# One more pair of contraction tiles per column pair in seven products, and another way to the sums of weights, in the down projection of a hybrid layer

## The reference, cut to what matters

```python
D_MODEL, SEQ, D_FF = 2048, 256, 5632

def conv_ffn(h, w_up, conv_w, conv_b, w_down):
    S = h.shape[1]
    u = h @ w_up
    up = jnp.pad(u, ((0, 0), (CONV_WIDTH - 1, 0), (0, 0)))
    u = sum(conv_w[j] * up[:, j:j + S] for j in range(CONV_WIDTH)) + conv_b
    a, b = jnp.split(u, 2, axis=-1)
    return (jax.nn.silu(a) * b) @ w_down

h = rms_norm(x, ffn_norm[l])
x = x + conv_ffn(h, w_ffn_up[l], ffn_conv_w[l], ffn_conv_b[l], w_ffn_down[l])
```

## Time and profile before

| | |
|---|---|
| median of 3 runs | 1081.04 us (1080.7 to 1081.21) |
| the profiled execution's own time | 1081.17 us |
| its span in the trace | 1079.4 us |
| PE busy in the span | 1074.4 us (100%), 6543 matmuls |
| PEld | 929.6 us (86%) |
| DVE | 906.8 us (84%) |
| ACT | 634.2 us (59%) |
| POOL | 85.4 us (8%) |
| granted TensorE clock | full speed in all slices |

### The profile page before, as it was taken

The page is one execution under the profiler, slowest core; times in us unless marked ns, Lnnn a source line. Parts: engine busy times, 40 slices in busy tenths (PEclk is TensorE's granted clock), DMA queues, the critical chain, the costliest instruction groups (busy, mean ns, idle before and its releaser), DMA issues.

```text
span 1079.4 us, 18186 instructions
## 1 busy us (share of the span) xinstructions
PE 1074.4 (100%) x6543; PEld 929.6 (86%) x6543; DVE 906.8 (84%) x1370; ACT 634.2 (59%) x930; POOL 85.4 (8%) x120
## 2 busy tenths in 40 slices
PE   9999999999999999999999999999999999999998
PEld 9888888888888888888888888888888888888887
DVE  7878988889756678888888888888878889999997
ACT  7677666757454655545555555555555566656663
POOL 4500100000000000000000000000000000000000
PEclk9999999999999999999999999999999999999999
DMA  8656879787889989888987988889798789789883
GB/s 276 181 162 198 201 231 237 210 225 219 244 262 268 242 269 232 236 251 251 248 245 243 243 242 259 228 246 292 238 257 233 213 292 335 266 309 330 273 308 143
DMA packets 191376, 265.49 MB, mean 246 GB/s; under 512 B 9797, under 2 KB 144086, under 8 KB 191062
## 3 DMA queue, kind: packets, MB, share of 16 engines
q1 hardware_dynamic: 173014, 217.81, 61.5%
q0 software_dynamic: 15616, 41.95, 19.9%
q10 hardware_dynamic: 2688, 5.00, 1.2%
HBM read 259.74 MB, written 46.92 MB: 284 GB/s over the span
## 4 chain that ended last, share of the span: by engine, by line
PE 99%; DVE 0%; issue 0%; DVEq 0%
PE bank L1824 38%; PE bank L1832 20%; PE bank L2219 7%; PE bank L2217 7%; PE bank L2218 7%; PE bank L2070 3%; PE bank L1871 3%; PE bank L1873 3%; PE bank L2072 3%; PE bank L1872 3%; PE bank L2071 3%; PE bank L1792 1%; PE bank L1900 1%; PE bank L2109 0%; PE bank L1797 0%; PE bank L1989 0%
## 5 line engine op out<-in xcount | busy, mean ns | idle before, releaser
L794 ACT CAST w_hi<-raw 128x1024 fp32r<-128x1024 f32 x299 | 312.8, 1050 | 254.3 <-PE bank L1832 114.8
L1203 DVE TENSOR_TENSOR w_lo<-raw,w_hi 128x1024 fp32r<-128x1024 f32 x299 | 364.2, 1223 | 107.7 <-ACT w_hi L794 107.2
L1824 PE MATMUL bank<-hs,w_hi 128*128 128x512 f32 x1792 | 423.0, 391 | 0.0
L1824 PEld LDWEIGHTS bank<-hs,w_hi 128*128 128x128 f32 x1792 | 331.3, 188 | 66.3 <-issue 0.9
L1832 PEld LDWEIGHTS bank<-hs,w_lo 128*128 128x128 f32 x1792 | 224.6, 191 | 5.6 <-issue 0.2
L1832 PE MATMUL bank<-hs,w_lo 128*128 128x256 f32 x1792 | 227.3, 283 | 0.0
L1173 ACT CAST hi_slot<-slot 128x1024 fp32r<-128x1024 f32 (+1 forms) x102 | 118.0, 1187 | 65.7 <-DVE slot L1749 23.5
L1730 DVE TENSOR_TENSOR slot_lo<-slot,hi_slot 128x1024 fp32r<-128x1024 f32 (+1 forms) x102 | 136.7, 1388 | 6.6 <-ACT hi_slot L1173 5.5
L2219 PE MATMUL bank<-hi_slot,gated 128*128 128x512 f32 (+1 forms) x194 | 75.1, 387 | 0.0
L2217 PE MATMUL bank<-hi_slot,gated 128*128 128x512 f32 (+1 forms) x194 | 75.1, 387 | 0.0
L1648 DVE SCALAR_TENSOR_TENSOR C<-U,cols,C 128x256 f32<-128x256 f32 x176 | 73.4, 480 | 0.0
(11 more groups left out here) (249 smaller groups left out, 1178.8 us busy)
## 6 DMA issues: line engine op xcount, KB each, us to landing
raw<-in_w_ffn_up_dram SPq DMA_DIRECT2D x176, 512.0 KB, 5.4
u_sums<-in_w_ffn_down_dram POOLq DMA_DIRECT2D x72, 512.0 KB, 6.8
raw<-in_w_in_dram SPq DMA_DIRECT2D x51, 512.0 KB, 4.7
slot<-u_sums SPq DMA_DIRECT2D x80, 256.0 KB, 5.9
slot<-in_w_ffn_down_dram SPq DMA_DIRECT2D x38, 512.0 KB, 5.1
raw<-in_w_in_dram SPq DMA_DIRECT2D x66, 256.0 KB, 3.5
raw<-in_w_out_dram SPq DMA_DIRECT2D x32, 512.0 KB, 5.8
slot<-in_w_ffn_down_dram SPq DMA_DIRECT2D x32, 256.0 KB, 4.2
```

The source lines that it names most:

```text
L794: act.copy(w_hi[:, i, :], raw[:, i, :]).then_inc(units_hi, 1)
L1203: dve.tensor_tensor(w_lo[:, i, :], raw[:, i, :], w_hi[:, i, :].bitcast(F32), ALU.subtract)\
L1824: m = pe.matmul(banks[b][:, :], w_hi[:, i, c], hs[:, 4 * i + k, :], start=(first and k == 0), stop=(final and k == 3))
```

## The change

It turns one eight of each column pair into a seven, so that 17 of 22 k-pairs are sevens instead of 16. Column pair 0 has 17 sevens in a row. In column pair 1, three runs of sevens (six, six, five) stand between eights, and the last seven is step 20 instead of 19. Three k-pairs' activation sums are parked instead of two, used in turns 6 to 8 of the sevens instead of 5 and 6, and x2's parts are loaded later. The weight sums are the same but made otherwise: in DRAM lie sum 1 = B11 + B12 and sum 2 = B21 + sum 1 for every k-pair, sum 3 = B11 + B21 for nine of 17. VectorE makes sum 3 for the others as sum 2 - B12 and sum 4 as sum 2 + B22, which do not depend on each other. POOL issues 86 transfers instead of 80, one in three units instead of three in ten, with a pause of eight units at unit 30. Piece "b" takes its two weight blocks from two tiles (rows of 2 KB) instead of one (4 KB). Small tiles move into shared ones.

```diff
-PATTERNS = ["CCCCSSSSSSSSDSSSSSSSSc", "CcSSSDSSSSSSSDSSSSSSCc"]
+PATTERNS = ["CCCCSSSSSSSSSSSSSSSSSc", "CcSSSSSSDSSSSSSDSSSSSc"]
-SECOND_SUM_IN_DRAM = tuple(range(0, 16, 2))
-LAST_PARKED_TURN = 6
+THIRD_SUM_IN_DRAM = tuple(range(0, 17, 2))
+LAST_PARKED_TURN = 8
-FIRST_SUM_QUAD = Q_F0
-SUM_STEP = (10, 3)
+SUM_STEP = (3, 1)
+FIRST_SUM_UNIT, SUM_PAUSE = 20, (30, 38)
-        X2_BACK_AT = [[5, 14, 17, 20], [13, 15, 17, 19]]
+        X2_BACK_AT = [[15, 17, 19, 20], [14, 16, 18, 19]]
...
-                sp.dma_start(raw_of(q, "a")[:, 0, :], w_down_v[:, 2 * n, out_columns(pair, 1)]).then_inc(a_loaded, 16)
-                sp.dma_start(raw_of(q, "a")[:, 1, :], u_sums_v[n, 1, :, pair, :]).then_inc(a_loaded, 16)
+                sp.dma_start(raw_of(q, "a")[:, 0, :], u_sums_v[n, 0, :, pair, :]).then_inc(a_loaded, 16)
+                sp.dma_start(raw_of(q, "a")[:, 1, :], w_down_v[:, 2 * n + 1, out_columns(pair, 0)])\
+                    .then_inc(a_loaded, 16)
                 wait_for_slot(q, "b")
-                sp.dma_start(raw_of(q, "b")[:, 0:2, :].rearrange("p b m -> p (b m)"),
-                             w_down_v[:, 2 * n + 1, out_both(pair)]).then_inc(b_loaded, 16)
-                sp.dma_start(raw_of(q, "b")[:, 2, :], u_sums_v[n, 0, :, pair, :]).then_inc(b_loaded, 16)
+                sp.dma_start(raw_of(q, "b")[:, 0:2, :], w_down_v[:, 2 * n:2 * n + 2, out_columns(pair, 1)])\
+                    .then_inc(b_loaded, 16)
+                sp.dma_start(raw_of(q, "b")[:, 2, :], u_sums_v[n, 1, :, pair, :]).then_inc(b_loaded, 16)
...
-                    dve.tensor_tensor(t2, t1, b21, ALU.add).then_inc(t2_made, 1)
-                    dve.wait_ge(t2_made, second_sums_made(q))
-                dve.tensor_tensor(t4, t2, b22, ALU.add).then_inc(t4_made, 1)
+                    dve.tensor_tensor(sum_3, sum_2, b12, ALU.subtract)
+                dve.tensor_tensor(sum_4, sum_2, b22, ALU.add).then_inc(sums_of_block_made, 1)
```

More of the change, by code:

```diff
@@ L429, in seven_of, with third_sum_in_dram, third_sums_loaded @@
             return pair * SEVENS + SEVEN_AT[pair].index(at)
-        def second_sum_in_dram(q):
+        def third_sum_in_dram(q):
             pair, at = divmod(q, QUADRUPLES)
-            return is_seven(pair, at) and K_PAIR_AT[pair][at] in SECOND_SUM_IN_DRAM
-        def second_sums_loaded(q):
-            n = sum(second_sum_in_dram(m) and SLOT_OF[m] == SLOT_OF[q] for m in range(OLD_RING, q + 1))
+            return is_seven(pair, at) and K_PAIR_AT[pair][at] in THIRD_SUM_IN_DRAM
+        def third_sums_loaded(q):
+            n = sum(third_sum_in_dram(m) and SLOT_OF[m] == SLOT_OF[q] for m in range(OLD_RING, q + 1))
             return 16 * n
-        def second_sums_made(q):
-            return sum(is_seven(*divmod(m, QUADRUPLES)) and not second_sum_in_dram(m) for m in range(q + 1))
         def pieces_of(q):
@@ L751, in wait_for_step @@
             def wait_for_step(step):
-                pool.wait_ge(units_used, FIRST_SUM_QUAD * RING + step * SUM_STEP[0] // SUM_STEP[1] + RING)
+                unit = FIRST_SUM_UNIT + step * SUM_STEP[0] // SUM_STEP[1]
+                if unit >= SUM_PAUSE[0]:
+                    unit += SUM_PAUSE[1] - SUM_PAUSE[0]
+                pool.wait_ge(units_used, unit + RING)
             def column_block(tile, c):
@@ L1733, in sums_of_weights @@
             def sums_of_weights(pair, at):
-                q, s = q_of(pair, at), seven_of(pair, at)
-                b21, b22, t1 = [raw_of(q, "b")[:, m, :] for m in range(3)]
-                t2, t4 = [raw_of(q, "c")[:, m, :] for m in range(2)]
+                q = q_of(pair, at)
+                b12, b22, sum_2 = [raw_of(q, "b")[:, m, :] for m in range(3)]
+                sum_3, sum_4 = [raw_of(q, "c")[:, m, :] for m in range(2)]
                 wait_for_down(dve, q, "b")
-                if second_sum_in_dram(q):
-                    dve.wait_ge(second_sum_loaded[SLOT_OF[q]], second_sums_loaded(q))
+                if third_sum_in_dram(q):
+                    dve.wait_ge(third_sum_loaded[SLOT_OF[q]], third_sums_loaded(q))
                 else:
```

67 lines of the change are left out of this document (31 added, 36 removed).

## The result

| | before | after |
|---|---|---|
| median of 11 runs each, one beside the other | 1081.06 us | 1084.42 us |
| lowest to highest | 1080.7 to 1082.26 | 1082.61 to 1087.44 |
| the profiled execution | 1081.17 us | 1083.33 us |
| its span | 1079.4 us | 1081.6 us |

The ratio is 1.0034 (95% interval 1.0026 to 1.0041): slower by over 0.2%. Two things stand out: the profiled execution is 1.1 us faster than the median, and the times lie three times as far apart as before.

The account below looks back on a forecast made before the run. It took TensorE, never starved in the down projection, as the bound, with VectorE nearly as full: 1081.17 - 1.36 + 2.11 + 0.8 = 1082.7 for the profiled execution, 1082.6 us for the median, range 1081.2 to 1084.2.

Parts of the forecast that it names:

- The matmuls that go: Down projection on TensorE: one product less per column pair, 6 matmuls at 0.2269 us, all on the path, -1.36 us.
- What costs nothing: Earlier stages: six more GpSimd transfers, the third parked set and moved small tiles fall where TensorE never waits, 0 us.
- one late unit: Earlier stages: if the cover failed, it would cost about what a landing wait does, up to 0.9 us.
- The tail: End of the kernel: VectorE's merge is no longer hidden, so the last addition starts 0.75 us later; +2.11 us.
- Behind it are the same stores: End of the kernel: after VectorE's last addition the stores were taken as unchanged, with no cost of their own.
- VectorE against TensorE: Down projection: VectorE loses its lead in the runs of sevens and TensorE stalls, +0.8 us, between 0 and 2.6.
- the cap: Down projection: landing loads cap VectorE's lead, so a kernel with less lead meets these waits less; argued against a 2.6 us stall.
- (2): Column pair 0's 17 sevens: VectorE falls behind as landing waits come as before, stall 2.6 us, 1084.4 us; chance 0.20.
- (3): Down projection: VectorE's two sums stay 0.72 us apart, 1.3 us more stall, 1083.9 us; chance 0.10.
- (1): Down projection: the whole gain arrives, 1.36 us less TensorE work is 1.36 us less time, 1079.7 us; chance 0.09.

Follow-up runs that it names:

- before_earlier: The kernel before with one of GpSimd's 80 transfers, the accumulating one due at unit 113, moved to unit 112; 1081.95 us, beside 1081.31 for the kernel before.
- one_later: The changed kernel with one of GpSimd's 86 transfers, the accumulating one due at unit 112, moved to unit 114; 1082.31 us, ratio 1.0008.
- look3: The changed kernel with nothing altered, one more profiled execution; 1086.53 us.
- doubled: The changed kernel with one more GpSimd transfer, a plain 512 KB copy straight behind the accumulating one of unit 112; 1085.77 us, ratio 1.0043.

## Why the prediction was wrong, step by step

**The matmuls that go: right.** 1.36 us, and the kernels without the other costs show it.

**What costs nothing: this is the step that failed.** It put GpSimd's transfers at nothing, under a cover, "stretches where TensorE never waits and VectorE idles 107.7 us ahead of its splits", and bounded one late unit by 0.9. The cover is an average over the stages. At 370 us there is none, as two rows of the kernel before, which the prediction did not look at, show:

```profile
370.27 1.28 DVE L1611 TENSOR_TENSOR xt<-xt,bank 128x512 f32<-128x512 f32 x2
```

```profile
371.60 1.09 PE L1792 MATMUL bank<-ident,xt 128*128 128x128 f32 x8
```

The additions end at 371.55 and TensorE's transposes start at 371.60: no slack, and ahead of the additions stand splits of loads just issued. The slack lay in the loads alone: issued at 358.20 and 359.97, ahead of the transfer at 360.43, they took 5.4 and 5.3 us and had landed 1.7 and 2.7 us before their casts began. The price failed too, because the earlier trace rows are waits for loads among loads. Behind the accumulating transfer at 356.6 the loads take 9 to 11 us instead of 4.5. The kernel before shows such a price as well: its load issued at 362.36, 1.9 us behind the transfer, takes 8.3 us and lands some 0.15 us ahead of its cast:

```profile
370.81 1.05 ACT L794 CAST w_hi<-raw 128x1024 fp32r<-128x1024 f32 x1 [1.71 <-PE bank L1832]
```

In the traces of the changed kernel that cost 0.8 to 2.7 us, once 1.6 more by the clock, and 2.1 in the median (1084.42 against 1082.31), where the prediction allowed up to 0.9.

The same schedule also gives something back early. In the kernel before, an accumulating transfer issued at 119.39 has a load behind it that takes 7.46 us, and TensorE has the 0.5 of "issue" in the earlier trace rows at 126.7. In the changed kernel neither is there, and its splits gain 0.75 us at 130 us. That the gap comes from that transfer was not tested. Another 0.4 us of the earlier start is no gain of the change: in this trace of the kernel before, the transposes that start at 5.89 us take 2.37 us, and in `before_earlier`, the same kernel up to there, 1.75.

**The tail: the additions right, the stores missed.** "Behind it are the same stores" is the second step that failed. The five stores were priced from the last addition. Before, they are issued over 3.3 us with a pause of 1.4 ahead of the third; after, 0.6 apart without a pause, and they wait for each other's packets (DMA share 1.1, and with fewer bytes the end comes 1.4 earlier). From the first issue to the last landing it is 5.69 and 5.75 us, so here the end follows the first store, which moved by 3.2, and not the last addition, which moved by 2.2. The term was +2.11 and measured 3.26 (12.26 - 9.0).

**VectorE against TensorE: mechanism right, size too large.** Column pair 0's run used up the lead (0.06 left at step 20), the sums are 0.60 apart, and there is no landing wait near the end of that run, where the lead is small: that was the cap. The stall was 0.25 in the first trace and 0.2 to 0.6 in all, where 0.8 stood.

**The sum in the profiled execution:** 1081.17 - 1.2 (earlier start without a late load, 856.86 of `one_later` against 858.05) - 1.36 + 3.26 + 0.25 + 1.2 (late load, 856.86 to 858.07) = 1083.3, against 1083.33.

**The rivals.** (2) gave 1084.4, the median to 0.02, by a mechanism that did not happen: its stall of 2.6 was 0.25. A right number is no proof. (3) is out: 0.60. In the same rows the split that waits for the sums starts 0.71 behind them (900.69 to 901.40). The rule of the Trainium skill, "VectorE: DVE Perf Modes", section "The DRAIN you can't avoid", that a semaphore costs nothing extra, is not what these rows show, as far as they go: each pair that is 0.71 to 0.72 apart both waits for a signal and reads what the first operation wrote. (1) lacked the hidden tail; with it and without the late load, the gain arrives.

## What to carry to other kernels

Before you call a background transfer hidden, look at the loads issued in the few us behind it, and at what stands behind their splits in program order: the slack of that place counts, not a stage's idle time. When several stores end a kernel, ask how far apart they are issued: if they come close enough to wait for each other, the end is priced from the first store's issue and the bytes. When the times of a kernel begin to scatter, compare traces of several executions by the start of each stage, and move one suspect alone.

## What the runs showed of the hardware that was not expected

While the accumulating transfer runs, about as many packets of one queue pass as of the other. Packets, MB and share by queue in the changed kernel (q0 is GpSimd's, q1 that of the loads), from 361 to 363 us, and then from 366 to 368 without it:

```profile
q0 software_dynamic: 141, 0.29, 80.4%
q1 hardware_dynamic: 144, 0.15, 27.8%
```

```profile
q1 hardware_dynamic: 727, 0.72, 103.8%
```

So 144 of the loads' packets (1 KB, 62 ns each, and 46 when alone) pass beside 141 of the transfer's (2 KB, 182 ns each), and the loads get 0.07 MB per us instead of 0.36. The Trainium skill says in "DMA: Bandwidth & Descriptors", section "Queues, rings and completion order": each DMA engine goes round between the queues that have work, and drains a whole packet from one before it turns to the next. The equal counts agree with that; the order of the packets is not in these rows. The loads' queue, with the smaller and faster packets, gets the smaller share of the bytes.

Not every transfer is as harmful. Between 310 and 470 us of the same trace, loads issued up to 2.3 us behind an accumulating transfer take 4.7 to 9.5 us, and behind a plain copy of GpSimd 5.9 to 6.9. What makes the one at 356.64 the worst was not tested.

TensorE's clock fell to half (1.2 GHz) behind a wait of 2.74 us in one trace (look3), 1.4 us after TensorE had begun to work again, and did not in another with a wait of 2.65 (`doubled`).
